# Attention stage of a two-layer decoder step: every sample batch is scored one unit later, and its shares are turned and mixed in the unit after that

## The reference

```python
def fox_block(q, Fq, qpos, k, v, Ft, kpos):
    s = jnp.einsum("bqhd,bshd->bhqs", q, k) * (DH_C ** -0.5)
    s = s + jnp.swapaxes(Fq, 1, 2)[..., None] - Ft[:, :, None, :]
    s = jnp.where(qpos[:, None] >= kpos[None, :], s, -jnp.inf)
    return jnp.einsum("bhqs,bshd->bqhd", jax.nn.softmax(s, axis=-1), v)

def fox_sample(q, k, v, lf, cache_k, cache_v, cache_logf, page_table, l):
    kp = cache_k[l, page_table]      # 8 batches x 16 pages x 128 positions
    ...
    s_past = jnp.einsum("bqhd,bphd->bhqp", q, kp) * scale + Fq[..., None] - Ft[:, :, None, :P]
    s_new = jnp.einsum("bqhd,bkhd->bhqk", q, k) * scale + Fq[..., None] - Ft[:, :, None, P:]
    s_new = jnp.where(jnp.tril(jnp.ones((T, T), dtype=bool)), s_new, -jnp.inf)
    p = jax.nn.softmax(jnp.concatenate([s_past, s_new], axis=-1), axis=-1)
    return jnp.einsum("bhqp,bphd->bqhd", p[..., :P], vp) + jnp.einsum("bhqk,bkhd->bqhd", p[..., P:], v)
```

## Time and profile before

| what | us |
|---|---|
| median of 3 runs | 2761.3 (2757.09 to 2761.54) |
| profiled execution, its own time | 2762.99 |
| span of the profile, first to last instruction | 2761.3 |
| TensorE busy in the span | 2688.6 |
| attention of layer 0, from about 377.4 to 552.0 | 174.6 |
| attention of layer 1, from about 1732 to 1906 | 174 |

### The profile page before, as it was taken

How to read it: one execution, slowest core, us unless ns; L and a number is a source line. 1 busy time by engine, 2 the same in 40 slices (tenths; PEclk the granted TensorE clock), 3 DMA queues, 4 the chain that set the end, 5 groups by cost and what they waited for, 6 DMA issues and landing times. The chain is left out here.

```text
span 2761.3 us, 48567 instructions
## 1 busy us (share of the span) xinstructions
PE 2688.6 (97%) x20596; PEld 2504.3 (91%) x20596; DVE 1233.8 (45%) x2223; ACT 639.5 (23%) x1058; POOL 263.3 (10%) x330
## 2 busy tenths in 40 slices
PE   6999999999999999999999999999999999999998
PEld 4999976699999999999999999667999999999998
DVE  5725535647423423324357354455653242242344
ACT  4324334423111101000132432443220000000012
POOL 0100100020000000000111011001000000000010
PEclk9999989999999999999999999899999999999999
DMA  8541178731222221111134102896112111111111
GB/s 308 160 102 39 62 256 313 252 117 46 90 79 92 77 92 59 57 47 46 62 113 120 52 32 103 319 331 216 47 54 77 46 47 46 47 54 46 47 60 65
DMA packets 107449, 295.37 MB, mean 107 GB/s; under 512 B 19669, under 2 KB 32854, under 8 KB 105442
## 3 DMA queue, kind: packets, MB, share of 16 engines
q1 hardware_dynamic: 107074, 291.49, 31.0%
q0 software_dynamic: 160, 0.79, 0.1%
HBM read 269.61 MB, written 22.63 MB: 106 GB/s over the span
## 5 line engine op out<-in xcount | busy, mean ns | idle before, releaser
L307 PE MATMUL PS<-hH,whi 128*128 128x352 f32 x1632 | 531.9, 326 | 4.8 <-PEq L1604 2.9
L307 PE MATMUL PS<-hL,whi 128*128 128x352 f32 x1632 | 523.2, 321 | 0.0
L307 PE MATMUL PS<-hH,wlo 128*128 128x352 f32 x1632 | 522.8, 320 | 0.0
L307 PE MATMUL PS<-aH,whi 128*128 128x352 f32 x1344 | 438.6, 326 | 3.7 <-PEq L384 3.2
L307 PE MATMUL PS<-aL,whi 128*128 128x352 f32 x1344 | 431.5, 321 | 0.0
L307 PE MATMUL PS<-aH,wlo 128*128 128x352 f32 x1344 | 431.3, 321 | 0.0
L295 POOL CAST whi<-raw 128x1024 fp32r<-128x1024 f32 x158 | 167.3, 1059 | 1660.9 <-PE PS L307 1328.3
L307 PEld LDWEIGHTS PS<-hH,whi 128*128 128x128 f32 x1632 | 306.2, 188 | 12.3 <-issue 7.2
L307 PEld LDWEIGHTS PS<-hL,whi 128*128 128x128 f32 x1632 | 306.7, 188 | 0.0
L307 PEld LDWEIGHTS PS<-hH,wlo 128*128 128x128 f32 x1632 | 305.9, 187 | 0.0
L861 PE MATMUL PS<-aH,whi 128*128 128x352 f32 x912 | 303.5, 333 | 1.9 <-ACT F L1071 1.9
(11 more groups left out here) (370 smaller groups left out, 3568.8 us busy)
## 6 DMA issues: line engine op xcount, KB each, us to landing
KVp<-kv SPq DMA_DIRECT2D x256, 384.0 KB, 5.4
raw<-w_ff SPq DMA_DIRECT2D x128, 512.0 KB, 3.5
raw<-w_in SPq DMA_DIRECT2D x42, 512.0 KB, 3.5
wad_single<-w_ada SPq DMA_DIRECT2D x40, 512.0 KB, 3.5
wad<-w_ada SPq DMA_DIRECT2D x32, 512.0 KB, 5.3
x_spill<-x SPq DMA_DIRECT2D x2, 4224.0 KB, 12.9
wada<-w_first SPq DMA_DIRECT2D x8, 1024.0 KB, 7.6
raw<-w_out SPq DMA_DIRECT2D x16, 512.0 KB, 3.5
```

The source lines that it names most:

```text
L307: last = nc.tensor.matmul(PS[:, 3 * p + part, 0:CW], w[:, k, :], a[:, k, part * CW:(part + 1) * CW], start=k == 0 and w is wh and a is hig ...
```

## The change

Nothing is computed otherwise; only the order within the stage of attention differs. `scores(b)` moves from part 1 to part 2, that is from iteration 3b+1 to 3b+2. `past_turned(b)`, `new_turned(b)` and `past_mixed(b)` move to iteration 3b+3: `past_turned` right behind the query-key products, the other two behind the turn. `new_turned` gets a bank of its own, where it had columns in the bank of a `mixed`, and its own semaphore is gone. The statistics move from iteration 23 to 24, and `turn_weights` and `pick` both come in iteration 25. Two copies of `mix_tile` on GpSimd move from iterations 18 and 20 to 16 and 17, and two subtractions on VectorE from 20 and 22 to 19 and 22.

```diff
-    LAST = 3 * NB - 1
-    assert LAST + 2 == NU + 1
+    LAST = 3 * NB
+    assert LAST + 1 == NU + 1
...
@@ GpSimd
-                    if i in (2 * CH + 2, 2 * CH + 4):
+                    if i in (2 * CH, 2 * CH + 1):
                         pool.wait_ge(S["low"], 4 * CH)
-                        k = (i - 2 * CH) // 2 - 1
+                        k = i - 2 * CH
@@ TensorE, new_turned on its own
-                def new_turned(b, at_):
+                def new_turned(b):
+                    key = ("new turned", b)
+                    has_room(pe, key)
                     pe.wait_ge(S["pad"], b + 1)
-                    return nc.tensor.transpose(PS[0:NS, at_, 2 * P:3 * P], PN[:, b, :], ident)
+                    nc.tensor.transpose(PS[0:NS, bank[key], 0:P], PN[:, b, :], ident).then_inc(S["filled"], 1)
...
-                    pe.wait_ge(S["new_out"], b + 1)
+                    is_empty(pe, ("new turned", b))
@@ TensorE, the loop
+                    b, part = divmod(i, 3)
+                    if 1 <= b <= NB and part == 0:
+                        past_turned(b - 1)
                     if i == LAST:
                         turn_stats()
-                    b, part = divmod(i, 3)
                     if b < NB and part == 2:
-                        past_mixed(b)
-                    if b < NB and part == 1:
                         scores(b)
                     if 1 <= i <= NU:
                         turn(i - 1)
                     if i == 1:
-                        first_turned()
+                        first_inverse()
+                    if 1 <= b <= NB and part == 0:
+                        new_turned(b - 1)
+                        past_mixed(b - 1)
+                    if i == LAST + 1:
+                        turn_weights()
                     if i >= 2:
                         mixed(i - 2)
-                    if b < NB and part == 1:
-                        past_turned(b)
                     if i == 0:
                         new()
                     if i == LAST + 1:
-                        turn_weights()
-                    if i == LAST + 2:
                         pick()
@@ VectorE, the loop
                     if i == LAST:
                         gather_stats()
-                    b, part = divmod(i, 3)
                     if b < NB and part == 2:
-                        past_mixed(b)
-                    if b < NB and part == 1:
                         scores(b)
                     if 1 <= i <= NU:
                         turned_copy(dve, nc.vector.tensor_copy, "dve", i - 1)
...
+                    if 1 <= b <= NB and part == 0:
+                        new_turned(b - 1)
+                        past_mixed(b - 1)
+                    if i == LAST + 1:
+                        pick_weights()
                     if i >= 2:
                         mixed(i - 2)
                     if i < NU:
                         dve.wait_ge(S["exp"], 2 * i + 2)
                         invert(i)
-                    if i in (2 * CH + 4, 2 * CH + 6):
-                        k = (i - 2 * CH) // 2 - 2
+                    if i in (2 * CH + 3, 2 * CH + 6):
+                        k = (i - 2 * CH) // 3 - 1
@@ ScalarE, the loop
+                    b, part = divmod(i, 3)
+                    beside = b < NB and part == 2
+                    if 1 <= b <= NB and part == 0:
+                        past_turned(b - 1)
+                    if i < NU:
                         exps(i, 0)
-                    b, part = divmod(i, 3)
-                    beside = b < NB and part == 1
                     if beside:
                         exps(i, 1)
...
-                    if b < NB and part == 1:
-                        past_turned(b)
```

More of the change, by code:

```diff
@@ L1526, in slot_table @@
                         take(("forget", i // CH, e, half), "act" if e else "dve")
+            b, part = divmod(i, 3)
+            if 1 <= b <= NB and part == 0:
+                take(("past turned", b - 1), "act")
             if i == LAST:
                 take(("stats",), "dve")
-            b, part = divmod(i, 3)
             if b < NB and part == 2:
-                take(("past mixed", b), "dve")
-            if b < NB and part == 1:
                 take(("scores", b), "dve")
@@ L1538, in slot_table @@
             if i == 1:
-                take(("new turned", 0), "dve")
+                take(("first inverse",), "dve")
+            if 1 <= b <= NB and part == 0:
+                take(("new turned", b - 1), "dve")
+                take(("past mixed", b - 1), "dve")
+            if i == LAST + 1:
+                take(("weights",), "dve")
             if i >= 2:
                 take(("mixed", i - 2), "dve")
-            if b < NB and part == 1:
-                take(("past turned", b), "act")
             if i == 0:
                 take(("new",), "dve")
-            if i > LAST:
-                take((("weights",), ("picked",))[i - LAST - 1], "dve")
+            if i == LAST + 1:
+                take(("picked",), "dve")
     slot_table()
@@ L1580, in attention @@
     def attention(l):
-        names = ("filled", "act", "dve", "qk", "low", "exp", "inverted", "new_out", "chain", "zero", "query", "cumulated", "fill", "min", "past_exp", "pad",
+        names = ("filled", "act", "dve", "qk", "low", "exp", "inverted", "chain", "zero", "query", "cumulated", "fill", "min", "past_exp", "pad",
                  "past_mixed", "gap", "share", "weights", "selected", "masks", "rows")
@@ L1717, in mixed @@
                                                     PT[piece[u, e, k // 4] % 6][:, k % 4, :], start=k == 0, stop=k == qb, skip_group_check=True)
-                    b, part = divmod(u + 2, 3)
-                    if part == 1 and b < NB:
-                        last = new_turned(b, bank[key])
                     last.then_inc(S["filled"], 1)
@@ L1755, in past_turned, with first_inverse @@
                     last.then_inc(S["filled"], 1)
-                def first_turned():
-                    key = ("new turned", 0)
+                def first_inverse():
+                    key = ("first inverse",)
                     has_room(pe, key)
-                    turn_inverse(0, bank[key])
-                    new_turned(0, bank[key]).then_inc(S["filled"], 1)
+                    turn_inverse(0, bank[key]).then_inc(S["filled"], 1)
                 def turn_inverse(u, at_):
@@ L1903, in invert, with new_turned @@
                     nc.vector.reciprocal(sums[:, i % 4, :], sums[:, i % 4, :]).then_inc(S["inverted"], 1)
-                def new_turned(b, at_):
+                def new_turned(b):
+                    key = ("new turned", b)
+                    is_full(dve, key)
                     if b >= 2:
                         is_full(dve, ("past mixed", b - 2))
-                    return nc.vector.tensor_copy(PTn[b % 2][:], PS[0:NS, at_, 2 * P:3 * P]).then_inc(S["new_out"], 1)
+                    nc.vector.tensor_copy(PTn[b % 2][:], PS[0:NS, bank[key], 0:P]).then_inc(S["dve"], 1)
                 def take_inverse(u, at_):
@@ L1916, in mixed @@
                     is_full(dve, key)
-                    b, part = divmod(u + 2, 3)
-                    if part == 1 and b < NB:
-                        new_turned(b, bank[key])
                     if u + 1 < NU:
@@ L1981, in _ @@
                     if i == 1:
-                        is_full(dve, ("new turned", 0))
-                        new_turned(0, bank["new turned", 0])
-                        take_inverse(0, bank["new turned", 0]).then_inc(S["dve"], 1)
+                        is_full(dve, ("first inverse",))
+                        take_inverse(0, bank["first inverse",]).then_inc(S["dve"], 1)
+                    if 1 <= b <= NB and part == 0:
+                        new_turned(b - 1)
+                        past_mixed(b - 1)
+                    if i == LAST + 1:
+                        pick_weights()
                     if i >= 2:
```

9 lines of the change are left out of this document (4 added, 5 removed).

## The result

| | us |
|---|---|
| before, median (20 runs) | 2761.09 (2756.64 to 2765.31) |
| changed, median (20 runs) | 2764.34 (2759.73 to 2769.45) |
| ratio changed to before | 1.0014, 95% interval 1.0007 to 1.0020 |
| forecast | 2752, range 2743 to 2761 |

The change makes the kernel slower by 0.14%, 3 to 4 us, within the 0.2% named in the prediction. The forecast was 9 us faster. The profiled execution of the changed kernel spans 2763.8 us, 2.5 more than before.

A forecast was written before the change was run, and what follows sets the result against it. TensorE, busy 2688.6 of 2761.3 us, was taken as the bound, with only its waits and clock in attention counting. Each layer's stage would end at 537.6 + 9.6 = 547.2 against 552.0, saving 9.6 in two layers: 2752, range 2743 to 2761.

The forecast's parts named there:

- 0.2% named in the prediction: Whole kernel: a difference within 5.5 us can't be told from no change; that outcome got 0.23.
- The start: Attention's start: first weighing at 398.6 instead of 398.89 us, one unit later in order, full clock assumed after 387.6.
- The loop: Weighing, page reads, last score step, next weighing: middle cycles 13.7 + 0.75 + 5.6 = 20.05 us; last weighing at 537.6.
- The first: First cycle between weighings: 24 tiles loaded ahead, so set by TensorE's work, 19.6 us.
- Other edits: Bank waits behind turned copies taken as 0, at most 0.3 us a batch; mix copies, if uncovered, 2 us a layer.
- The last: Last cycle: pages 12.8 us after the weighing, cycle 18.7 us, plus 0.4 for VectorE's late copies of unit 23.
- The end: Last weighing to end of `pick`: 9.6 us instead of 12.4, with mixed(23) starting 2.65 us after mixed(22).
- Rival A: Clock falls again at attention's start, 10 us at half clock costing 5 us a layer: no change, 2761; chance 0.10.
- The casts: End of attention: GpSimd's casts, loaded before the last weighing, are over when VectorE weighs the batches, its last product 0.28 us.
- Rival C: Tiles return a turn later, lengthening the loop: pages at 14.9 us give 2766, deciding from 14.5 us; chance 0.10.
- B: Pages land sooner, the loop does not bind, cycles are 19.0 us of TensorE work: 2741; chance 0.16.
- D: New order adds unseen waits, at bank turns or VectorE after weighing, 0.5 us in 16 batches: 2760; chance 0.14.

The follow-up runs named there:

- fill_wait: Changed kernel with 16 idle transposes filling most of TensorE's wait before `turn_weights`: 2761.58 us, ratio 1.0001 to the kernel before.
- weigh_early: Changed kernel with VectorE's `weigh_batches` moved ahead of the last batch's picked rows: 2756.17 us, ratio 0.9977 to the kernel before.
- half_after: Changed kernel reading only the keys of pages from ring step 6 on, half the bytes, sample outputs wrong: 2746.54 us, ratio 0.9942 to the kernel before.
- sums_late: weigh_early with SP's read of forget values moved behind the second step's pages of its batch: 2759.37 us, ratio 0.9992 to the kernel before.
- half_before: Kernel before, reading only the keys of pages from ring step 6 on, half the bytes, sample outputs wrong: 2754.87 us, ratio 0.9975.
- sums_late_before: Kernel before with SP's read of forget values moved behind the second step's pages of its batch: 2761.18 us, ratio 0.9999.
- late_weights: Against weigh_early: old order shifted one unit, new-position turn just before weighing, `weigh_batches` again behind mixed(22): 2756.53 us.
- turn_added: Like late_weights, but `weigh_batches` early and the prompt unit's turn again between scores and weighing: 2761.39 us, ratio 0.9997 to the kernel before.

## Why the prediction was wrong

Two steps of it failed: the price of the loop, which was too low at both of its ends and in layer 1, and the wait at the end of the stage, which was taken at full clock. By the pair of traces the loop is the larger: 9.0 us in the cycles of both layers, against 3.0 us at the ends of the stage.

**The start** seems to hold: 20.3 us into the stage for the first weighing in layer 0, forecast 20.4; the wait for VectorE was 1.9 us, forecast 1.6. In layer 1 it was 21.8, since the second stretch of half clock shrank to 3.4 us there and did not vanish. But the 20.3 is luck of this execution. Five kernels have this start (the changed one, fill_wait, weigh_early, half_after, sums_late), and in their ten stages the first weighing comes 19.8 to 22.4 us into the stage, mean 21.2. In the six stages of the kernel before, half_before and sums_late_before it comes at 20.7 to 21.7, mean 21.0. So no gain at the start is shown, where 0.3 us a layer were forecast. The time at half clock there did shrink, to 3.4 to 13.7 us, mean 7.8, from 10.2 to 17.1, mean 15.4; why the first weighing is no sooner for it was not traced.

**The loop** is the first step that failed. Its middle held in layer 0: for pages 13.7 us were taken, and 13.2 to 13.8 was measured; cycles of 20.05 were forecast, and from the second weighing to the seventh (416.88 to 517.68) they were 20.2. In layer 1, which the forecast took to be as layer 0, the pages came 13.4 to 14.5 us after the weighing, and the same five cycles (1773.30 to 1877.43) took 20.8 us each, the last of them 22.6. And the forecast drew its gain from the two cycles at the ends, which were priced by other rules. The first, "set by work, 19.6 us", took 20.1: ScalarE's copies were late by 0.3 us twice, work that was put at 0 under "Other edits". The last, priced at 18.7 and 0.4 because nothing is read behind the last pages, took 20.5. Its pages came 13.65 us after the weighing (531.33 - 517.68), not 12.8, and behind the scores stood 0.87 us for VectorE. The first cycle is 0.5 us over, the five in the middle 0.5 together, the last 1.4, which is 2.4; with the start that is 2.3 us in layer 0. The comparison that should have been made is cycle by cycle with the kernel before. There, too, the pages came 13.3 to 14.9 us after the weighing, but TensorE had one turn more to do until then and one less behind the scores. The experiments measure it: one turn moved from the one half of the loop to the other costs 8 to 13 us. weigh_early bears out by its median that start and loop together are the larger part of the miss: with the two waits of 2.1 us gone, the prediction's own sum would give it 2748, and it took 2756.17, though no half clock is left at its ends.

**The end** is the second step that failed. The wait before `turn_weights` was seen and priced right: mixed(23) was to start 2.65 us after mixed(22), and it was 545.24 - 542.98 = 2.3. Rival A held that an idle time of 1.6 us might bring the clock down, but only at the start; the 2.65 us at the end were taken as time alone. Without the 1.8 us of half clock that fill_wait shows, the end would have been 9.3 us, against 9.6 forecast; at most 1.1 us more a layer lies behind it, in the next stage.

**VectorE beside the cast.** The casts were said to be over by the time that VectorE weighs the batches. That is so, but they then fell on `gather_stats`, whose last product took 1.14 us instead of 0.28. With it the copy that the last weighing waits for came 0.86 us later, as much as the wait of 0.87 us above:

```profile
536.80 1.14 DVE L1943 TENSOR_TENSOR share<-top,both 8x128 f32<-8x128 f32 x1
537.87 0.87 DVE L1855 COPY PT<-PS 128x128 f32<-128x128 f32 x2
538.66 0.27 DVE L1913 COPY PTn<-PS 32x128 f32<-32x128 f32 x1
```

The cast on GpSimd ran from 536.76 to 537.80. The Trainium skill (GPSIMD Engine Reference, "1. Specifications") names contention with VectorE instructions that have two SBUF inputs; the product has two such inputs, and the trace agrees: 1.14 us beside the cast, 0.28 on the same shape alone. Other traces show what decides it. In layer 1 of the changed kernel and of sums_late and in layer 0 of half_after, the cast starts 0.02 to 0.04 us ahead of the product, the product takes 1.12 to 1.16 us, and TensorE waits 0.86 to 0.90 us. In fill_wait the product starts 0.04 us ahead of the cast in layer 0 (539.56 and 539.60); it takes 0.28 us, and TensorE does not wait. The same holds in both layers of weigh_early. So this 0.9 us hangs on hundredths of a microsecond.

**Sum,** by the one pair of traces. With 4.8 us off, layer 0 should have been 175.2 - 4.8 = 170.4 us long and was 173.8: 2.3 us up to the last weighing, 1.5 at the end, -0.4 at the change of stage. Layer 1 should have been 169.3 and was 178.3: 1.4 at the start, 6.6 in the cycles (the 2.95 us wait and the half clock of batch 6 among them), 1.5 and -0.4. Together that is 12.4 us, and 12.3 lie between forecast and median.

Rival C named the mechanism of the loop but set its point of decision at pages of 14.5 us. They didn't need to be that late in all cycles: gains at the ends of the loop that weren't there, and the clock, used up most of the 4.8 us with pages at 13.6 in layer 0, and in layer 1 one batch did come at 14.5. B did not happen here and is what half_after shows. D's waits are real: at the turn of the new positions and ahead of the weighing ScalarE's copies are late four times, 0.35, 0.45, 0.35 and 0.23 us in layer 0, behind the scores, where they count in full.

**Left open.** Why pages take 13 us and more after a weighing, and why the clock fell for 3.4 us in some cases, for 10.2 in others and not at all in others, was not settled. The copies of `mix_tile` with their subtractions, and the bank of its own for `new_turned`, were not tried alone; none of TensorE's waits above comes from them.

## What to carry to other kernels

When a ring of tiles is freed by one piece of work and fed for another, read the loop in two halves: what stands between release and next use is cover for the transfer, what stands behind it is added to the cycle. A piece of work that moves from the one half to the other can cost up to its length in each cycle, though the total work is the same: here a turn of some 1.15 us, moved in 14 cycles, cost 8 to 13 us. And a wait of some 2 us on TensorE may cost more than its length: put the granted clock of the stretch behind it into the sum, wherever the wait is; VectorE's small operations for such a wait belong into the time in which VectorE stands anyway.

## What was not expected of the hardware

The half clock behind a wait had no fixed length in these runs. 2.13 us of idle brought 10.2 us at 0.50 at both ends of the changed kernel; 2.07 us in late_weights brought none in layer 0 and 6.8 in layer 1; 2.95 us in batch 6 brought 3.4. Nor did length alone decide: 1.96 us in layer 1 of weigh_early had 3.4 us at half clock behind it, 2.05 us in layer 0 of the changed kernel and 2.19 us in layer 0 of turn_added had none. Where TensorE waits for pages, they arrive 12.9 to 15.5 us after the weighing, whichever order with full reads it is; moving the one read of forget values, 256 KB a batch, did not bring them sooner.
